# An encoder layer on one core: the normalised x's block operands stored split in the first gate stage and loaded split by the next two

## The reference

```python
xn = rms_norm(x, norm_mix_w)
rq, rk, rv, rg, cq, ckv, kpe, ga, gb = split_columns(xn @ w_in)
...
ret_y, mla_y, new_state = mixer_core(rq, rk, rv, q, ckv, kpe, w_ukv)
ret_branch = (head_group_norm(ret_y, ret_gn_w) * silu(rg)) @ w_ret_o
mla_branch = mla_y @ w_mla_o
merged = sigmoid(ga) * ret_branch + sigmoid(gb) * mla_branch
h = x + merged @ w_out
g, u = split(rms_norm(h, norm_ffn_w) @ w_gate_up, 2)
h = h + (silu(g) * u) @ w_down          # then a final rms_norm
```

## Time and profile before

| | us |
|---|---|
| median of 3 runs | 2066.67 |
| profiled execution, its time | 2069.99 |
| its span | 2067.8 |
| PE busy | 1996.2 (97%) |
| VectorE busy | 1290.7 (62%) |
| ScalarE busy | 788.4 (38%) |
| six octets, first to last matmul | 758.1 to 1307.0 |

### The profile page before, as it was taken

How to read it: one execution, slowest core, us unless ns; L and a number is a source line. 1 busy time by engine, 2 the same in 40 slices (tenths; PEclk the granted TensorE clock), 3 DMA queues, 4 the chain that set the end, 5 groups by cost and what they waited for, 6 DMA issues and landing times.

```text
span 2067.8 us, 35131 instructions
## 1 busy us (share of the span) xinstructions
PE 1996.2 (97%) x14160; PEld 1925.6 (93%) x14160; DVE 1290.7 (62%) x2026; ACT 788.4 (38%) x1382; POOL 531.3 (26%) x424
## 2 busy tenths in 40 slices
PE   8999999999999989999999979999999999999997
PEld 8978888889989989899999979899999999999997
DVE  6567776765666556866667996755555656432257
ACT  5334445442222235455544425544343434210010
POOL 0110000001344442324224141144444454200000
PEclk9999999999999999999999989899999999999998
DMA  8301010151444466764755442123232322763412
GB/s 312 112 24 32 24 32 25 32 218 50 140 167 165 166 230 214 259 219 163 246 203 193 169 151 102 69 86 126 85 119 93 107 104 96 270 231 116 170 54 87
DMA packets 114241, 282.37 MB, mean 137 GB/s; under 512 B 13345, under 2 KB 30689, under 8 KB 106529
## 3 DMA queue, kind: packets, MB, share of 16 engines
q1 hardware_dynamic: 114080, 280.12, 38.5%
HBM read 191.85 MB, written 88.23 MB: 135 GB/s over the span
## 4 chain that ended last, share of the span: by engine, by line
PE 82%; DVE 12%; issue 2%; ACT 2%; DMA 1%; POOL 1%; SPq 0%; DVEq 0%; ACTq 0%; POOLq 0%
PE ps L1157 25%; PE ps L1158 24%; PE ps L1159 24%; PE ps L1252 1%; DVE t_lo L2140 1%; PE ps L1350 1%; DVE tmp L2147 1%; DVE negmax L2369 1%; PE ps L1258 1%; DVE s_lo L2140 1%; PE ps L1466 1%; PE ps L1413 1%; DVE pt_lo L2140 1%; PE ps L1409 1%; PE ps L1410 1%
## 5 line engine op out<-in xcount | busy, mean ns | idle before, releaser
L1157 PE MATMUL ps<-s_hi,t_hi 128*128 128x272 f32 x1344 | 393.6, 293 | 18.9 <-DVE s_lo L2140 18.1
L1158 PE MATMUL ps<-s_hi,t_lo 128*128 128x272 f32 x1344 | 391.9, 292 | 0.0
L1159 PE MATMUL ps<-s_lo,t_hi 128*128 128x272 f32 x1344 | 390.8, 291 | 0.0
L1157 PE MATMUL ps<-sx_hi,t_hi 128*128 128x272 f32 x1232 | 357.3, 290 | 0.1
L1158 PE MATMUL ps<-sx_hi,t_lo 128*128 128x272 f32 x1232 | 357.1, 290 | 0.0
L1157 PEld LDWEIGHTS ps<-s_hi,t_hi 128*128 128x128 f32 x1344 | 257.9, 192 | 21.7 <-DVE s_lo L2140 14.5
L1159 PEld LDWEIGHTS ps<-s_lo,t_hi 128*128 128x128 f32 x1344 | 257.7, 192 | 0.0
L1158 PEld LDWEIGHTS ps<-s_hi,t_lo 128*128 128x128 f32 x1344 | 257.6, 192 | 0.0
L1159 PE MATMUL ps<-sx_lo,t_hi 128*128 128x272 f32 x880 | 255.2, 290 | 0.0
L1157 PEld LDWEIGHTS ps<-sx_hi,t_hi 128*128 128x128 f32 x1232 | 235.1, 191 | 0.4 <-DVE t_lo L2140 0.2
L1158 PEld LDWEIGHTS ps<-sx_hi,t_lo 128*128 128x128 f32 x1232 | 234.7, 190 | 0.0
(11 more groups left out here) (281 smaller groups left out, 4963.1 us busy)
## 6 DMA issues: line engine op xcount, KB each, us to landing
t_row<-in_weights SPq DMA_DIRECT2D x48, 512.0 KB, 5.7
y_spill<-hg_r SPq DMA_DIRECT2D x44, 544.0 KB, 3.4
yd<-y_spill SPq DMA_DIRECT2D x22, 1088.0 KB, 5.6
s_raw<-s_x SPq DMA_DIRECT2D x21, 1088.0 KB, 5.7
w_stage<-in_weights SPq DMA_DIRECT2D x35, 512.0 KB, 3.9
raw<-in_weights SPq DMA_DIRECT2D x22, 512.0 KB, 5.2
hg<-in_weights SPq DMA_DIRECT2D x22, 512.0 KB, 5.2
d_stage<-in_weights SPq DMA_DIRECT2D x24, 384.0 KB, 3.1
```

Source lines behind the costliest of these rows:

```text
L1157: nc.tensor.matmul(out, wh, xh, start=start, stop=False, skip_group_check=onto)
L1158: nc.tensor.matmul(out, wl, xh, start=False, stop=False, skip_group_check=onto)
L1159: return nc.tensor.matmul(out, wh, xl, start=False, stop=stop, skip_group_check=onto)
```

## The change

The first gate stage still loads `s_raw` and splits it. When a step of it starts, SyncE also stores that step's `s_hi` and `s_lo`, 1088 KB each, to a new HBM tensor `x_split`. The steps of GATE_A and GATE_B (`presplit(j)`, 14 steps) load both parts into `s_hi` and `s_lo` directly, and nothing is split for them: 28 instructions go on ScalarE and 28 on VectorE. PE waits for the load of both parts instead of for `so_low`. A buffer whose store is under way must not be overwritten, so the load three steps later waits for the landing of both stores (`split_out`, semaphores that were in use earlier). `splits_before(j)` renumbers the counts of `so_high` and `so_low`.

```diff
 def loads_until(j):
-    return sum(loaded(i) for i in range(j % 3, j + 1, 3))
+    return sum(loaded(i) * (2 if presplit(i) else 1) for i in range(j % 3, j + 1, 3))
+
+def presplit(j):
+    return STEPS * GATE_A <= j < STEPS * BRANCH_RET
+
+def splits_before(j):
+    return sum(not presplit(i) for i in range(j))
...
+        x_split = nc.dram_tensor("x_split", (STEPS, 2, P, 4, HALF), F32, kind="Internal").ap()
...
+        split_out = list(zip((cache_landed, cache_ckv_in, tables_in, spill_out, gain_in, consts_in, prep_in),
+                             (16, 16, 64, 2 * KT * 16, 16, 48, 256)))
...
 (operand_turn)
-            return STEPS * o + s + 1, p - 1
+            return None if presplit(STEPS * o + s + 1) else (STEPS * o + s + 1, p - 1)
...
 (operand_load)
                 if j > 2:
                     sp.wait_ge(oct_done, 4 * (j - 2))
+                if 0 <= j - 3 < STEPS:
+                    sp.wait_ge(split_out[j - 3][0], split_out[j - 3][1] + 32)
+                if presplit(j):
+                    for i, dst in enumerate((s_hi[j % 3], s_lo[j % 3])):
+                        sp.wait_ge(split_out[s][0], split_out[s][1] + 32)
+                        sp.dma_start(dst[:, :, :].bitcast(F32), x_split[s, i]).then_inc(s_in[j % 3], 16)
+                    return
...
 (octet_transfers)
                     if p == 0 and j < STEPS * OCTETS and loaded(j):
                         operand_load(j)
+                    if p == 0 and o == GATE_RET:
+                        sp.wait_ge(so_low, 2 * splits_before(s) + 2)
+                        for i, src in enumerate((s_hi[s % 3], s_lo[s % 3])):
+                            sp.dma_start(x_split[s, i], src[:, :, :].bitcast(F32)).then_inc(split_out[s][0], 16)
...
 (octet_unit, on PE)
-                            pe.wait_ge(so_low, 2 * j + k // 2 + 1)
+                            if presplit(j):
+                                pe.wait_ge(s_in[j % 3], 16 * loads_until(j))
+                            else:
+                                pe.wait_ge(so_low, 2 * splits_before(j) + k // 2 + 1)
...
 (operand_octet_low; residual_added and up_sums alike)
-                dve.wait_ge(so_high, 2 * j + part_of + 1)
+                dve.wait_ge(so_high, 2 * splits_before(j) + part_of + 1)
```

More of the change, by code:

```diff
@@ L2535, in residual_added @@
                 if c == C22:
-                    dve.wait_ge(so_low, 2 * (STEPS * o + 3) + p // 2 + 1)
+                    dve.wait_ge(so_low, 2 * splits_before(STEPS * o + 3) + p // 2 + 1)
                 dve.wait_ge(m_sum, m_sum_at(BRANCH_MLA, "S4" if c == C12 else "S2", p))
@@ L2563, in up_sums @@
                         dve.wait_ge(sm_out[6], SM_OUT)
-                        dve.wait_ge(so_low, 2 * (STEPS * MIX_OUT + 2))
+                        dve.wait_ge(so_low, 2 * splits_before(STEPS * MIX_OUT + 2))
                     nc.vector.tensor_tensor(s3_raw[:, p, :], acc(C11, p), acc(C21, p), ALU.subtract).then_inc(s_sum_p, 1)
```

## The result

The changed kernel has a median of 2080.24 us (2078.48 to 2081.70, 4 runs), the kernel before 2066.74 in the same comparison (4 runs). The ratio is 1.0067, 95% interval 1.0054 to 1.0081: +13.9 us, 11.2 to 16.7. It is slower, inside the predicted range and 5.2 us above the predicted time.

The account below looks back on a forecast made before the run. PE was taken to bound the kernel. The landing of C12's last store at 883.2, then 1.95, 12.03 and 2.0 us, put step 10 at 899.2 instead of 890.9: +8.3 on 2066.7 gives 2075 us, range 2060 to 2084.

Parts of the forecast that it names:

- PE-bound, with all that can be gained at one seam: PE busy 1996.2 of 2067.8 us; it waits only at the seam of the first two stages, where 9.6 us are lost.
- The relief: At the seam, taking operands 7 to 9's splits off VectorE removes four PE idle times, worth at most 9.6 us.
- Splits beyond step 9: Splits of steps 10 to 20, behind which PE never waits: removing them is worth 0.
- L: Landing of C12's last store, which ScalarE's unit 32 copy awaits: 883.2 by bytes issued ahead at 404 GB/s, before 872.95.
- The clock after the idle time: PE's clock is low after its wait before unit 36; 2.0 us lost, taken from the octets' start.
- The waits that I put at 0: Operand 9's load, C11's last store and the last weight row come late, but only shorten idle before unit 36: 0.
- one sign that I had named for being wrong: At the seam, PE not being idle at 875 would show the forecast wrong.
- The other signs: No s_lo wait from 840 to 880, low clock after PE's idle, landings of 15 us or more or SyncE held.
- Full gain: Rival at the seam: transfers fit, L at most 867.4, all four waits go, -9.6 us, 2057; chance 0.17.
- The draw: Rival at the seam: fewer MB in the way, L from 871 to 876, -4 to +1 us, 2063 to 2068; chance 0.15.
- nothing: Rival: VectorE's other work holds the seam, L under 875, within 2 us of 2066.7; chance 0.05.
- The rival at 358 GB/s: Rival: the seam's long queue runs at the octet's full-share rate, L = 894.1, +19.2 us, 2086; chance 0.08.

Follow-up runs that it names:

- e3: Changed kernel without x_split stores, one load per step, GATE_A and GATE_B splitting nothing (numbers differ from the reference): 2060.58 us, ratio 0.9964 to the kernel before.
- e6: Changed kernel with only operands 7, 8 and 9 stored and loaded split, and s_yg stores ahead of their unit's operand load: 2059.83 us, ratio 0.9965 to the kernel before.
- e5: Whole change, with GATE_A's lagging s_yg stores issued ahead of the same unit's operand load: 2075.25 us, ratio 1.0043 to the kernel before.
- e8: Whole change, each x_split store carrying two of four blocks, loads reading s_x (numbers differ from the reference): 2070.72 us, ratio 1.0022 to the kernel before.
- e1: Changed kernel with x_split stores and landing waits kept, but all stages loading s_x and splitting: 2074.01 us, ratio 1.0036 to the kernel before.
- e2: Changed kernel without x_split stores, both parts loaded from s_x, GATE_A and GATE_B splitting nothing (numbers differ): 2066.11 us, ratio 0.9997 to the kernel before.
- e4: Changed kernel with only operands 7, 8 and 9 stored and loaded split, all others split as before: 2064.75 us, ratio 0.9986 to the kernel before.
- e9: Kernel before with only GATE_A's lagging s_yg stores issued ahead of the unit's operand load: 2066.11 us, ratio 0.9993 to the kernel before.
- e7: Changed kernel with GATE_A splitting and storing, and only GATE_B loading split: 2078.82 us, ratio 1.0048 to the kernel before.

## Why the prediction was right, and where its sizes were off

**PE-bound, with all that can be gained at one seam.** Shown. With the splits gone and no transfer added the waits on `s_lo` vanish (e3). The relief was put at 9.6 and measures 7.4 (interval 4.5 to 10.1), which holds it and lies below it in the middle. Splits beyond step 9 were put at 0: e6, which takes off only three operands, gains as much as e3, which takes off fourteen.

**What sets the loss: L, the landing of C12's last store.** Shown from both sides: e5 makes the same transfers with the result stores of GATE_A's units ahead of the loads and gets 5 us back; e8 takes bytes away ahead of them and gets 9 back; e1 has L at 876.0 as counted with the 384 GB/s that the changed kernel had shown. Unit 36 at L + 1.95 measured L + 1.93. The prediction's own formula says that the change is zero at L = 875.0, which is 116.9 from the octets' start. With the copies of the table above it gives +14.3 for the changed kernel, +10.4 for e5 and +3.5 for e8, each 0.5 more by the clock below; the seams show +14.8, +11.3 and +4.1.

**The size of L.** Predicted 883.2, measured 887.54: the term that was off, by 4.3 of the 4.8 us between the predicted and the traced step 10 (899.2 and 903.98). The rate was nearly as put. With my 2.0 us of latency taken off, the engines moved 400 GB/s up to L, where I had put 404:

```profile
798.90:887.50 88.60, 70.83 (x548) 70.17 (x546) 52.95 (x70) 29.96 (x47) 11.65 (x8) 0.92 1.02 400
887.54:893.00 5.46, 3.54 (x15) 3.54 (x16) 3.94 (x4) 4.24 (x8) 2.78 (x2) 0.50 0.46 193
```

The bytes were. I let 34.0 MB pass, all that is issued up to C12's last store, and nothing behind it. From 796.9 to 887.5 the engines moved 393 GB/s x 90.6 us = 35.6 MB. Behind that store SyncE issued one more result store (875.73) and both loads of operand 11 (877.60, 878.09), 2.5 MB, and after L only 193 GB/s x 5.46 us = 1.05 MB of them were still to be moved. So about 1.5 MB issued behind the store were moved before it had landed, 3.6 us at 400 GB/s; the rate of 400 in place of 404 is most of the rest. The order of issue isn't strict: load 11's high part landed at 889.2, 1.7 us after the store. That the bound I gave, 386 with L = 887.2, met the value is luck: 34.0 MB in 88.4 us are 385 GB/s, but the queue ran at 400. The 429 of the upper bound stands in one slice of the earlier trace rows, not in several.

A second part shows when L is counted from the octets' start: predicted 125.1, measured 131.2, 6.1 us off and not 4.3. SyncE was already held when my count begins. Step 5's load went out at 796.91, 40.6 us after the octets' start and not 39.0 as before, since it waited for the landing of step 2's low part (issued at 785.27, 11.6 us). I had this wait in the change and counted from 797.1 as if it cost nothing.

**The clock after the idle time.** Put at 2.0 from the earlier trace rows. Step 10 began 903.98 - 889.47 = 14.51 us after unit 36, 2.5 more than the 12.03 of an undisturbed step. The granted clock from 889.4 to 894.4 was 0.50, the lower of its two levels (1.2 of 2.4 GHz), and half of 5 us are 2.5.

**The start.** Step 10 is 13.04 us later, but from a common start the loss is 14.8, since the octets of the profiled execution of before began 1.8 us later. The forecast was 8.3; of the 6.5 us that it lacked L gives 6.1 and the clock 0.5. The medians' +13.9 (11.2 to 16.7) agrees with 14.8.

**The waits that I put at 0.** The copy of unit 28 was held to 861.25, not 857: C11's last store was issued at 843.72, right behind four transfers of 1088 KB, and took 17.5 us to land. PE idled 7.73 us before 863.17. It adds nothing, as predicted: PE has only units 32 to 35 to run before it waits for L anyway. But one sign that I had named for being wrong did show: PE wasn't idle at 875. It ran those units until 877.57, not 870, so its idle time before unit 36 was 11.90 us; unit 36 hung on L all the same. The other signs came as told: no wait on a `s_lo`, landings above 15 us, a low clock behind. Load 9 was issued at 861.53 in place of 856.4, as step 6's low part landed at 860.5 only, with the queue full behind it. GATE_B with two loads per step and PE 100.00 of 100.00 us busy is as forecast.

**The rivals.** Full gain needed 34 MB by 867.4; the queue didn't move them. A gain exists with 9 transfers of 1088 KB added in place of 28 and the store ahead of the load (e6). The draw and "nothing" needed L near or under 876, and it was 887.54. The rival at 358 GB/s (+19.2) fell: the mean at a full queue was 393 and the late windows 408. So the sentence of the Trainium skill (DMA: Bandwidth & Descriptors, section "Where 436 GB/s comes from") that the HBM side binds at about 358 doesn't hold for this core. Another page of the Trainium skill (HBM Reference, section "Specifications (TRN2)") says that a core streaming alone measures well above that share; this trace agrees, with 393 and 408 GB/s.

**A step missing from the prediction** showed in e2 and e4. SyncE, held at its issues by a full queue, reached C12's last store 106.0 and 105.5 us after the octets' start, where it was 103.2 with a shorter queue (e3), and load 10 ahead of it passes first. Taking that load from in front gave 2.7 us of L (113.9 in e4, 111.2 in e6), as much as its 1.1 MB take at 404 GB/s. I looked for relief in fewer bytes and found it only with the order changed as well.

## What to carry to other kernels

Storing a result of work so that later stages can skip the work trades an engine for the DMA queue. Before judging it, find the small transfer that someone waits for, count all bytes issued ahead of it and, as this order isn't strict, some of those issued right behind it (here 1.5 MB), and divide by the rate of a full queue. Do it only for the operands whose work stands in the way (here 3 of 14), and issue what is waited for ahead of what is only needed later; either measure alone gave at most -2.9 us, both together -7.2 us.

## What the runs showed of the hardware that I had not expected

- With the DMA queue deep, the issuing engine is held: 3.54 and 5.29 us for one issue (0.32 to 0.45 in a short queue). A 272 KB store took 13.0 us to land, another 17.5.
- Transfers issued up to 3.6 us behind a store were in part moved before it had landed: about 1.5 MB of 2.5.
- The rate at a full share isn't one number: 393 GB/s from 810.0 to 836.6, 408 from 875.9 to 887.5. The transfers differ (weight rows and pieces in the first, large loads and result stores in the second), but no run tests whether that is the cause.
- TensorE's granted clock over the 5 us after an idle time was 1.00 after 1.20 us (e6), 0.66 after 4.09 (e4) and 0.50 after 5.40 (e2), 10.20 (e8) and 11.90 us (the changed kernel). The length alone doesn't tell it: after 1.76 us it was 0.66 in the kernel before and 1.00 in e9, after 2.49 us 1.00 (e7), and after 7.73 us 0.61 (the changed kernel).
